# Keys and values turned by VectorE instead of TensorE, operands moved to 64 byte lines, and the loads ahead of a scan in another order

## What is computed

```python
def reference(x, meta_tokens, ...):
    h = concatenate([meta, x], axis=1)                 # (1, 1040, 1024)
    h = h + gla_mixer(rms_norm(h, gla_norm[0]), ...)   # gated linear attention, 4 heads
    h = h + gdn_mixer(rms_norm(h, gdn_norm[0]), ...)   # gated delta net, 8 heads
    return rms_norm(h, final_norm)[:, 16:]

def gdn_mixer(h, w_in, conv_w, a_log, dt_bias, head_norm, w_out):
    qkv, z, beta_logit, a_logit = split(h @ w_in)      # 2048, 2048, 2048, 8, 8 columns
    q, k, v = split(silu(causal_depthwise_conv(qkv, conv_w)))
    ...                                                # q, k normed, log_a from a_logit
    o = gdn_chunk_scan(q, k, v, sigmoid(beta_logit), log_a, s0, c)   # chunks: 16, then 64 tokens
    return (rms_norm(o, head_norm) * silu(z)) @ w_out
```

## Time and profile before

| | |
|---|---|
| three runs, median | 1447.57 us (1446.95 to 1448.4) |
| the profiled execution's own time | 1450.41 us |
| its span | 1448.5 us |
| mean granted clock of TensorE | 0.996 |
| TensorE busy, matmuls | 1423.2 us, 98% |
| VectorE, ScalarE, GpSimd busy | 757.0, 466.1, 412.3 us |
| moved by DMA | 200.35 MB in 213918 packets |

### The profile page before, as it was taken

One profiled execution on the slowest core, in us unless ns is written; L12 is line 12 of the kernel. 1 busy time (PEld: TensorE's weight loads), 2 busy tenths in 40 slices (PEclk: granted clock), 3 DMA queues, 4 the chain that ended last, 5 costly groups with the idle time before them and its releaser, 6 DMA issues.

```text
span 1448.5 us, 21451 instructions
## 1 busy us (share of the span) xinstructions
PE 1423.2 (98%) x8458; PEld 1198.8 (83%) x8458; DVE 757.0 (52%) x937; ACT 466.1 (32%) x958; POOL 412.3 (28%) x359
## 2 busy tenths in 40 slices
PE   8999999999999999999999999999989999999997
PEld 6878799878888899999999999888866777777776
DVE  5225522225553366455465687799934654444442
ACT  5325621133222253433334544321232622111121
POOL 3213134251110131122121177243342541222200
PEclk9999999999999999999999999999999999999999
DMA  5621244466554135444463232244378885555530
GB/s 191 187 81 58 76 153 150 157 235 198 182 175 142 47 88 128 110 109 122 121 197 98 76 92 79 83 125 137 117 262 208 237 230 154 145 141 158 167 88 29
DMA packets 213918, 200.35 MB, mean 138 GB/s; under 512 B 62873, under 2 KB 177065, under 8 KB 213570
## 3 DMA queue, kind: packets, MB, share of 16 engines
q1 hardware_dynamic: 207234, 187.53, 43.6%
q10 hardware_dynamic: 6592, 11.54, 2.9%
HBM read 131.93 MB, written 67.09 MB: 137 GB/s over the span
## 4 chain that ended last, share of the span: by engine, by line
PE 55%; DVE 6%; ACT 2%; DMA 1%; issue 1%; DVEq 0%; POOLq 0%; ACTq 0%; POOL 0%
PE banks L2195 17%; PE banks L3011 13%; PE banks L2272 12%; DVE gdn L2529 4%; PE banks L3067 2%; PE banks L3100 2%; PE banks L3072 2%; PE banks L2089 2%; PE banks L3081 1%; PE banks L2113 1%; PE banks L3055 1%; PE banks L3024 1%; DMA gdn_z<-gdn 1%; ACT gdn L2328 1%; ACT gdn L2350 1%
## 5 line engine op out<-in xcount | busy, mean ns | idle before, releaser
L2195 PE MATMUL banks<-hn_hi,gdn 128*128 128x352 f32 x1488 | 309.6, 327 | 0.0
L2195 PEld LDWEIGHTS banks<-hn_hi,gdn 128*128 128x128 f32 x1488 | 244.5, 188 | 4.4 <-issue 2.7
L2195 PE MATMUL banks<-hn_lo,gdn 128*128 128x352 f32 x744 | 168.1, 321 | 0.0
L2272 PE MATMUL banks<-gdn,hn_hi 128*128 128x512 f32 x512 | 165.1, 403 | 1.8 <-ACT gdn L2475 1.5
L2529 DVE SCALAR_TENSOR_TENSOR gdn<-gdn,conv_taps,gdn 128x1040 f32<-128x1040 f32 x96 | 161.7, 1684 | 7.7 <-ACT gdn L2336 4.9
L2480 POOL TENSOR_TENSOR gdn<-gdn,gdn 128x1024 fp32r<-128x1024 f32 x31 | 84.4, 2722 | 268.4 <-ACT gdn L2311 268.4
L2195 PEld LDWEIGHTS banks<-hn_lo,gdn 128*128 128x128 f32 x744 | 127.3, 188 | 0.0
L920 PE MATMUL banks<-gdn,hn_hi 128*128 128x512 f32 x384 | 120.5, 395 | 0.0
L2272 PEld LDWEIGHTS banks<-gdn,hn_hi 128*128 128x128 f32 x512 | 96.7, 190 | 28.1 <-issue 3.0
L2272 PE MATMUL banks<-gdn,hn_lo 128*128 128x512 f32 x256 | 102.2, 399 | 0.0
L3011 PE MATMUL banks<-gdn,gdn 128*128 128x512 f32 x384 | 95.4, 397 | 1.4 <-DVE gdn L3226 1.2
(11 more groups left out here) (321 smaller groups left out, 2404.0 us busy)
## 6 DMA issues: line engine op xcount, KB each, us to landing
gdn<-in_gdn_w_in SPq DMA_DIRECT2D x32, 512.0 KB, 4.0
gdn<-in_x SPq DMA_DIRECT2D x16, 512.0 KB, 3.5
gdn<-in_gla_w_in SPq DMA_DIRECT2D x32, 256.0 KB, 4.2
gdn_kq<-gdn SPq DMA_DIRECT2D x16, 512.0 KB, 3.8
gdn_v<-gdn SPq DMA_DIRECT2D x16, 512.0 KB, 3.5
gdn<-in_gdn_w_in SPq DMA_DIRECT2D x32, 256.0 KB, 4.5
gdn<-gdn_kq SPq DMA_DIRECT2D x16, 512.0 KB, 3.8
gdn<-gdn_ek SPq DMA_DIRECT2D x16, 512.0 KB, 5.5
```

Of the source, the lines that this page charges most:

```text
L2195: return pe.matmul(acc[n % 2][:, b, 0:m], w[n % 2][:, kt, :], x[:, kt, PAD + s:PAD + s + m], start=(kt == 0 and e == 0), stop=(kt == KT - ...
L2272: mm = pe.matmul(z_bank(grp * TT + t), x[:, kt, P + t * P:P + (t + 1) * P], z_half(w, p_), start=(kt == 0 and e == 0), stop=(kt == KT - 1 ...
```

## The change

- k and v are turned by VectorE: `dve.transpose` on a whole tile of 128x1056 (1040 tokens, filled up to `LT`), which turns each block of 32 by 32 by itself, from SBUF to SBUF. The hooks `tr_k` and `tr_v`, their banks' copies and ScalarE's share are gone.
- Since the blocks lie in another order, `store_tok` puts them in place: four DMAs per tile, one for each 32 channels, of 1056 runs of 128 bytes.
- `SPANS` becomes 352, 352, 336. Buffers for fp32r start on 64 bytes (`LINE` = 16 floats), as do the arenas.
- `z_slot` is k % 4 for all z tiles, in buffers of their own; `z_lo(0)` waits for VectorE's fifteenth v tile.
- The inverses of the first two chunks are stored apart (`store_first`, 0.5 MB), chunk 0's are loaded, and then the 4 MB store goes out (`store_ua`). ScalarE waits for all of it ahead of chunk 0. GpSimd does the meta tokens' multiply by beta.
- The scan's first loads stand in another order (k and v of meta ahead of its inverse, z ahead of chunk 1's inverses), and GpSimd's meta step stands ahead of `decayed(0)`.
- The last output projection writes to banks 0 and 1 and does not wait for the residual before it.

```diff
-SPANS = [(0, 352), (352, 344), (696, 344)]
+SPANS = [(0, 352), (352, 352), (704, 336)]
+TB = 32
+LT = -(-L // TB) * TB
...
             def store_tok(dst, buf, c, sem):
-                sp.dma_start(dst[0:NMETA, c:c + P], buf[0:NMETA, 0, :]).then_inc(sem, 16)
-                sp.dma_start(dst[NMETA:L, c:c + P].rearrange("(t p) c -> p t c", p=P), buf[:, 1:NT, :]).then_inc(sem, 16)
+                for i in range(P // TB):
+                    sp.dma_start(dst[:, c + i * TB:c + (i + 1) * TB].rearrange("(j t) c -> t j c", t=TB),
+                                 buf[i * TB:(i + 1) * TB, :].rearrange("t (j c) -> t j c", c=TB)).then_inc(sem, 16)
...
-            def ev_v(i, b):
-                dve.wait_ge(S("ni_vtr"), 3 * i + b + 1)
...
+            def ev_v(i):
+                dve.wait_ge(S("ni_silu"), nth(v_tile(i)) + 1)
+                dve.wait_ge(S(f"ni_tok_out{i % 2}"), STORES * (NH // 2 + i // 2))
+                dve.transpose(tok[i % 2][:, :], vT_of(i)[:, :]).then_inc(S("ni_vev"), 1)
...
             def z_lo(p_):
+                if p_ == 0:
+                    pool.wait_ge(S("ni_vev"), NV // P - 1)
...
-                if n >= v_tile(2) and kt in (0, 1, 5):
-                    tr_v(v_of(n - 2), min(kt, 2))
...
         def z_slot(k):
 
-            return k % 4 if k < G3 * TT else 1 + k % 2
+            return k % 4
...
+        def store_first(sp):
+
+            sp.wait_ge(S("ni_u"), 2)
+            for c in range(FIRST):
+                sp.dma_start(T.gdn_ua_first[c], sc_x[c::NCH]).then_inc(S("ni_ua_out"), 16)
...
-            at = row.end
-            row.end = at + -(-math.prod(shape[1:]) // 8) * 8
+            size = math.prod(shape[1:])
+            unit = LINE if dt == F32R else 8
+            at = -(-row.end // unit) * unit
+            row.end = at + -(-size // 8) * 8
...
-        pY = [bank[:, 6 + n, :] for n in range(2)]
+        def pY(t, half):
+
+            return bank[:, (6 if t < TT - 1 else 0) + half, :]
...
-                wait(pe, S("ns_yd"), 2 * t)
+                if t < TT - 1:
+                    wait(pe, S("ns_yd"), 2 * t)
```

More of the change, by code:

```diff
@@ L1852, in st_of @@
             return H.st if n == 2 else st[n % 2]
-        vT = [late.take([P, L]) for j in range(2)]
-        hi = [late.take([P, KT, P], F32R) for j in range(2)]
-        lo = [late.take([P, KT, P], F32R) for j in range(2)]
+        v_first = late.take([P, LT])
+        hi_odd = late.take([P, KT, P], F32R)
+        late.end = LATE + 4128
+        hi = [late.take([P, KT, P], F32R), hi_odd]
+        lo_odd = late.take([P, KT, P], F32R)
+        lo = [late.take([P, KT, P], F32R), lo_odd]
+        vT = [v_first, late.take([P, LT])]
         x_at = late.end
@@ L1858, in gdn_in @@
         cv = late.take([P, L])
-        tok = [late.take([P, NT, P]) for j in range(2)]
+        tok = [late.take([P, LT]) for j in range(2)]
         assert late.end <= ARENA
@@ L1924, in z_half @@
             b = 1 - p_ % 4 // 2
+            if b and bufs is not st:
+                return (z_hi_odd if bufs is hi else z_lo_odd)[:, p_ % 2 * 4:p_ % 2 * 4 + 4, :].rearrange("p k c -> p (k c)")
             return bufs[b][:, p_ % 2 * 4:p_ % 2 * 4 + 4, :].rearrange("p k c -> p (k c)")
@@ L2780, in gdn_scan @@
         behind.end = ahead.end
-        St = behind.take([P, NH, NDV])
         oT_hi = behind.take([P, KO, P], F32R)
         oT_lo = behind.take([P, KO, P], F32R)
-        kq_at, ek_at, St_at = 0, 2 * NH * 2 * C, ahead.end
+        og = [behind.take([P, HP, NDV]) for n in range(2)]
+        h = [behind.take([P, D])]
+        hole = behind.end
+        behind.end = FRONT + 2 * C * C
+        assert behind.end == hole + D
+        kq_at, ek_at, St_at = 0, 2 * NH * 2 * C, behind.end
+        St = behind.take([P, NH, NDV])
         last_hi = A.at(St_at, [P, KO, P], F32R)
         last_lo = [A.at(n, [P, KO // 2, P], F32R) for n in (kq_at, ek_at)]
-        og = [behind.take([P, HP, NDV]) for n in range(2)]
         vn = behind.take([P, HP, NDV])
+        ua = [behind.take([P, HP, 2, C]) for n in range(2)]
         kt = [behind.take([P, HP, NDK]) for n in range(2)]
-        ua = [behind.take([P, HP, 2, C]) for n in range(2)]
-        h = [behind.take([P, D]) for n in range(2)]
+        h.append(behind.take([P, D]))
         junk = T.hn_hi_f32[:, :, D:TP]
@@ L2941, in chunk @@
                 if m == 2:
-                    for k in range(F.tiles + TT - 2, F.tiles + TT):
+                    for k in range(F.tiles + TT - 4, F.tiles + TT):
                         F.z_stored(sp, k)
@@ L3225, in residual @@
                 c = slice(half * 512, half * 512 + 512)
-                dve.tensor_tensor(h[t % 2][:, c], pY[half], h[t % 2][:, c], ALU.add).then_inc(S("ns_yd"), 1)
+                dve.tensor_tensor(h[t % 2][:, c], pY(t, half), h[t % 2][:, c], ALU.add).then_inc(S("ns_yd"), 1)
             def final(t):
@@ L3375, in gdn @@
 def gdn(nc, S, E, T, A, H, bank, w_in, w_out, head_norm, out_norm, out):
-    with nc.sbuf_tensor("gdn", [P, ARENA + 8], F32), nc.Block() as block:
+    with nc.sbuf_tensor("gdn", [P, ARENA + LINE], F32), nc.Block() as block:
         F = gdn_in(S, E, T, A, H, bank, w_in)
```

261 lines of the change are left out of this document (106 added, 155 removed).

## The result

The changed kernel takes **1424.76 us** (median of 4 runs, 1423.77 to 1425.95) where the kernel before took 1447.99 beside it. The ratio is 0.9839, 95% interval 0.9822 to 0.9856: 23.2 us faster. The forecast was 50 us, and 1424.76 lies 4.8 us outside the range.

The account below looks back on a forecast made before the run. TensorE was taken to pace the kernel, so work leaving its stream shortens it. Savings 30.1 - 4 + 13.8 + 9.0 + 1.15 = 50 us off 1447.6 gave 1397.6 us, range 1390 to 1420.

Parts of the forecast that it names:

- Step 1: k and v tiles: transposes leave TensorE, 23.8 us over 24 tiles, plus 6.3 us of silu waits; 30.1 us saved.
- Step 2: VectorE takes over the transposes; late v tiles tight, its lateness meets TensorE at the start of z; 4 us charged.
- Step 3: Operands on 64 byte lines: 4.6 ns per differently lying 512 column matmul, plus projections; 13.8 us saved, ends 0 and 15.
- Step 4: Hole ahead of the scan: 3.9 us of waits and 5.1 us of lower clock go; 9.0 us saved, low end 0.
- 5, the end: Last projection no longer waits for the residual; 1.15 us saved.
- the rival decided from 40 on: Tile stores: 128 byte runs choke the DMA engines, deciding from 40 ns a run; about 1501 us at 60; chance 0.05.
- list of signs: What would show the forecast, including block transpose at 1.1 to 1.5 us, z at 229 to 230 ns per matmul.
- the rival of a slow transpose: Late v tiles: VectorE becomes the bound, transpose at half pace; 9 us back, 1407, lower clock adds 5; chance 0.13.
- by analogy only: L1303, L1292 and half of L3011: about 800 matmuls with the stationary operand off the line; 3.7 us of step 3.
- this rival, at 0.12: Alignment does nothing on the chip; L920's two runs differ in bank too; 13.8 us back, 1411 us; chance 0.12.
- the hole stays in another form: Ahead of the scan: 4 MB store meets last z stores, or ScalarE awaits its landing; 1407 to 1412 us; chance 0.16.

Follow-up runs that it names:

- portions held: The changed kernel with no portion of the inverses issued behind the last two tiles, run behind the last v tile instead: 1415.21 us, ratio 0.9776.
- with the later store: The changed kernel with no inverse portions in the last two tiles and the 4 MB store behind the last z stores: 1416.96 us, ratio 0.9776.
- with the pieces: The changed kernel with inverse portions held back from the last two tiles and the 4 MB store issued as eight DMAs: 1415.7 us, ratio 0.9779.
- the last run: Changed kernel, portions held, 4 MB store late, 0.9 us inverse pieces in four VectorE gaps, GpSimd's inverse with its old stops: 1410.67 us, ratio 0.9744.

## Why the prediction was off

The sum by its own steps, forecast and measured in the two profiled executions (negative: faster):

| step | forecast | measured | from |
|---|---|---|---|
| 1, transposes off TensorE | -30.1 | -29.5 | 28.3 by the end of the tiles, less 1.3 of step 3, plus the packs that stood in z, 2.5 |
| 2, VectorE late at z | +4 | +9.9 | wait 7.8, lower clock 2.1 |
| 3, alignment | -13.8 | -2.7 | 0.4 ahead of the tiles, 0.9 in them, 0.3 in z, 1.1 in the scan |
| 4, the hole | -9.0 | -0.3 | waits 4.4 for 3.9; clock 4.3 for 5.1 |
| 5, the end | -1.15 | -1.4 | last projection and the transposes ahead of it 26.15 us, with the wait 27.6 before |

The sum is -24.0; the span gave -24.4, each row being good to some tenths of a microsecond. Steps 2, 3 and 4 fell short by 5.9, 11.1 and 8.7 us, which is the whole miss.

**Step 1** was right in mechanism and size. So was the bound on the DMA engines: 14.3 ns a run, where the rival decided from 40 on.

**Step 2** failed where it said that silu, transpose and low split "follow each other" behind the last tile and charged 4 us. These three were sized rightly, 3.8 us from the silu at 900.95 to TensorE's start, and the transpose was cheaper than charged, 1.27 us for 1.46. (The prediction's list of signs has 1.1 to 1.5 us for it; nothing measured gives the 1.1. The sixteen of v in the changed kernel took 1.21 to 1.28, and the 1.46 was an estimate from the copy in the earlier trace rows.) What was missed is that they do not start when TensorE ends: the fifteenth tile's convolution ended 3.9 us behind the last tile's matmuls, for a whole portion of the inverses, 6.8 us, was queued on VectorE ahead of it. Before, the fifteenth tile's packs stood between matmuls of z, so that z did not wait for them to begin; now convolution and transpose stand behind the portion and the low split behind the transpose. (That `z_lo(0)` waits for the fifteenth tile at all is part of the change, and no run took it away.) Taking the portions away in the last two tiles brought z 6.15 us forward; doubling the transposes moved it 5.9 back, 2.3 of it at z. I also left out the lower clock, which came with the wait of 7.8 us (0.50 to 0.51, for 6.8 us), though the text names it for the rival of a slow transpose.

**Step 3** was mostly wrong. The rule from the earlier trace rows (operands that lie differently against a 64 byte line cost 4.6 ns) does not hold even there: with both operands on the line L920's two runs took 232.9 and 233.3 ns. Nor does it carry over: z, all of the "off" kind, gained 0.5 ns a matmul when put on the line (125.07 us for 536, 233.3 ns, against 233.9). Only L1303, reckoned "by analogy only", paid fully (2.3 us), and even that is not seen whole: all that lies ahead of the tiles is only 0.4 us shorter in the profiled execution. For the projections the rule has the wrong shape, as the two halves alone each made the pieces shown slower by 1.5 to 1.7 ns. The two runs in the earlier trace rows differ in bank and weights too, as the rival said; this rival, at 0.12, was nearly right. What does set the pace stays open. The runs show only that it depends on places and spans jointly, and no run separated bank, weights and address.

**Step 4** failed in its timing. It put the end of VectorE's inverses some 8 us before TensorE reaches the meta step, and so the 4 MB store behind the last z stores. The inverses ended 27 us before (1031.9 against 1059.2): they began 8 us behind the start of z and not 15, and z took 154 us and not 143, since it runs at 233 ns and holds the low clock and the hole. So the store fell into the z stores, as the rival "the hole stays in another form" had it (chance 0.16). That the store makes the hole was right: with it moved, the hole and the lower clock went.

The rivals were listed one at a time and the range was made of two of them; three came together.

## What to carry to other kernels

When work moves from the bound engine to a free one, look at what is queued there ahead of the moved work and ahead of what it reads. Busy time 92% says little here; the one unbroken piece of 6.8 us in front explains most of the wait. A bulk store is a neighbour in time of whatever small transfers it meets (here z stores landed in 8.6 us beside it and in 2.7 without it, both medians): fix its place by an event on the other stream, for a speed-up upstream shifts both, and not by the same amount. And a pace difference between two runs of one line is not a rule until one factor alone has been changed.

## What the runs showed of the hardware

- A stream transpose of 128x1056 fp32 values took VectorE 1.27 us (mean of sixteen), less than the 1.42 us copy of 128x1024 inside SBUF.
- Runs of 128 bytes cost 14.3 ns of a DMA engine each (102912 more packets, 1469 us more), runs of 512 bytes about 30 ns (an estimate from q1's time before and after).
- Stores of 256 KB of z landed in 2.7 us with the 4 MB store moved behind them, and in 8.6 us (both medians of ten) with it issued among them; issuing that in eight pieces left 7.2 us for the median and 8.1 for the store on the chain.
- In a wait of 7.8 us the granted clock fell from 1.00 to 0.50 2.5 us before its end and stayed there for 4.3 us of work (the changed kernel). With waits of 3.5 and 0.9 us and short work between, it was at 0.50 for 10.2 us (the same run). After waits of 3.3 us it was at 0.50 for 3.4 us in two runs (portions held, alone and with the later store) and stayed at 1.00 in a third (with the pieces). After 2.8 us (the store in pieces) it stayed at 1.00, after 1.9 us (each tile turned twice) and 2.0 us (stores issued twice) it was at 0.50 for 3.4 us, and after 1.6 us it stayed at 1.00 in all three runs that have such a wait (portions held, with the later store, and the last run). So in these runs the length of the wait alone does not tell.
- The same three-span projection ran at 157.6 to 160.0 ns a matmul, depending on operand places and column spans together, and L920 at 229.2 to 233.8 ns with no rule found.
